# A decoder trunk on one core: the out-projections cut into sixteen more tiles, eight of them in the attention and SSD phases

## The reference

```python
up = rmsnorm(hp, norm_pre[i])
...
return (y * jax.nn.silu(gate)) @ w_out, bufs       # attention, y is 2048 wide
...
y = (yg.reshape(n, l, SSD_D_INNER) * norm_w.astype(jnp.float32)).astype(u.dtype)
return y @ w_out, h_new, conv_new                  # SSD, y is 2048 wide
...
hp = hp + rmsnorm(yp, norm_post[i])
```

## Time and profile before

| | us |
|---|---|
| runs, median of 3 (lowest, highest) | 1526.88 (1523.71, 1529.86) |
| the profiled execution's own time | 1523.6 |
| its span | 1521.8 |
| PE busy | 1368.0 (90%) |
| DVE busy | 815.2 (54%) |
| ACT busy | 670.8 (44%) |
| POOL busy | 454.4 (30%) |

### The profile page before, as it was taken

One profiled execution on the slowest core, in us unless ns is written; L12 is line 12 of the kernel. 1 busy time (PEld: TensorE's weight loads), 2 busy tenths in 40 slices (PEclk: granted clock), 3 DMA queues, 4 the chain that ended last, 5 costly groups with the idle time before them and its releaser, 6 DMA issues. The chain is left out here.

```text
span 1521.8 us, 29918 instructions
## 1 busy us (share of the span) xinstructions
PE 1368.0 (90%) x11182; PEld 1302.2 (86%) x11182; DVE 815.2 (54%) x1437; ACT 670.8 (44%) x1453; POOL 454.4 (30%) x393
## 2 busy tenths in 40 slices
PE   4999989999999998999966899499998989985996
PEld 4999879998899997999956899388897988874896
DVE  4444275443655445554443422667879769795323
ACT  3333433334434334343352432457566665743332
POOL 2545323453325442344420011002425143250011
PEclk8999999999999999999988899599999999997998
DMA  5562332623336233263421930443463735525711
GB/s 158 158 200 71 110 104 82 213 85 109 93 99 208 85 109 93 82 197 119 113 61 56 310 98 0 123 129 111 121 188 88 206 94 158 161 85 194 227 55 59
DMA packets 271172, 190.67 MB, mean 125 GB/s; under 512 B 10608, under 2 KB 258112, under 8 KB 270656
## 3 DMA queue, kind: packets, MB, share of 16 engines
q1 hardware_dynamic: 271040, 188.86, 41.5%
HBM read 159.92 MB, written 49.75 MB: 138 GB/s over the span
## 5 line engine op out<-in xcount | busy, mean ns | idle before, releaser
L1306 POOL TENSOR_TENSOR wlo<-w,whi 128x1024 fp32r<-128x1024 f32 x88 | 214.0, 2432 | 426.7 <-ACT whi L1001 426.7
L845 PE MATMUL at_proj<-uhi,whi 128*128 128x272 f32 x1408 | 310.8, 302 | 10.1 <-issue 6.1
L845 PE MATMUL at_proj<-uhi,wlo 128*128 128x272 f32 x1408 | 293.6, 290 | 0.0
L845 PE MATMUL at_proj<-ulo,whi 128*128 128x272 f32 x1408 | 293.3, 290 | 0.0
L845 PEld LDWEIGHTS at_proj<-uhi,whi 128*128 128x128 f32 x1408 | 221.6, 191 | 14.5 <-issue 7.4
L845 PEld LDWEIGHTS at_proj<-ulo,whi 128*128 128x128 f32 x1408 | 223.9, 191 | 0.0
L845 PEld LDWEIGHTS at_proj<-uhi,wlo 128*128 128x128 f32 x1408 | 222.9, 191 | 0.0
L1001 ACT ACTIVATE whi<-w 128x1024 fp32r<-128x1024 f32 x88 | 93.0, 1057 | 289.0 <-PE at_proj L845 272.1
L1740 PE MATMUL sd_proj<-uhi,sd_whi 128*128 128x272 f32 x640 | 143.7, 306 | 11.2 <-DVE sd_wlo L2134 11.2
L341 PE MATMUL m_acc<-m_yhi,m_whi 128*128 128x272 f32 x512 | 111.5, 300 | 35.8 <-DVE m_ylo L474 33.6
L1740 PE MATMUL sd_proj<-uhi,sd_wlo 128*128 128x272 f32 x640 | 134.5, 293 | 0.0
(11 more groups left out here) (296 smaller groups left out, 2517.4 us busy)
## 6 DMA issues: line engine op xcount, KB each, us to landing
w<-in_attn_w_in_dram SPq DMA_DIRECT2D x92, 512.0 KB, 4.0
sd_w<-in_ssd_w_in_dram SPq DMA_DIRECT2D x40, 512.0 KB, 4.4
m_rows<-mixed SPq DMA_DIRECT2D x32, 272.0 KB, 5.7
sd_h<-in_state_ssm_dram SPq DMA_DIRECT2D x16, 512.0 KB, 6.1
sd_bc<-acs_p SPq DMA_DIRECT2D x16, 512.0 KB, 5.3
out_s_ssm_dram<-sd_h SPq DMA_DIRECT2D x16, 512.0 KB, 3.1
m_w<-in_attn_w_out_dram SPq DMA_DIRECT2D x7, 1024.0 KB, 6.6
m_w<-in_ssd_w_out_dram SPq DMA_DIRECT2D x7, 1024.0 KB, 7.4
```

The lines of the kernel that those rows point to most:

```text
L845: last = pe.matmul(proj[:, r, h, 0:HALF], a[:, r, kk * P:(kk + 1) * P], b[:, kk, h * HALF:(h + 1) * HALF], start=(kk == 0 and a is whi and ...
L1306: pool.tensor_tensor(wlo[:, r], w[:, r], whi[:, r].bitcast(F32), ALU.subtract).then_inc(wlo_ready, 1)
```

## The change

Each out-projection is cut in two along its contraction. The first half, on the y of groups 0 and 1, becomes eight tiles of 1024 x 128 behind the projection stream: in attention as tiles of a group NG in the last stage, in SSD as tiles of kind "O". Their input is read back from `y_dram` into SBUF, split into `uhi` and `ulo` when the last projection is done (`split_high`, `split_low`; `YL`, `YH`), and their results stay in SBUF as `part`. In SSD `part` lies in the buffers `xbc` and `raw`. The second half, on groups 2 and 3, is done in `mix_phase`, with eight tiles of 48 products on the same ring. There DVE adds `part` in place of ACT's copy (`add_part`). Group 3's y (in SSD also group 2's) stays in SBUF and is neither stored nor loaded. The last tiles of each phase load and split the first two weight tiles of the next: those of the mix phases and, in `m1` on POOL, those of SSD. `all_groups` loops over two stages and writes the third out. The loops of `mix_phase` are written out. SSD's due times are new (two lines of the table are shown), and POOL now sums z of the last group as well.

```diff
 def all_groups(eng, plan, stage):
 
     stage(plan.first())
-    with eng.Fori(0, NG - 1) as i:
+    with eng.Fori(0, NG - 2) as i:
         stage(plan.middle(i))
+    stage(plan.middle(NG - 2))
     stage(plan.last())
...
+def out_tile(w_out, n):
+
+    k, o = divmod(n, KD)
+    return w_out.rearrange("(k p) n -> p k n", p=P)[:, KD * k:KD * (k + 1), o * P:(o + 1) * P]
...
+            for k in absent:
+                sp.dma_start(y[k], y_dram[KD + k]).then_inc(y_in, 16)
+            for o in range(PAIR, 2 * PAIR):
+                load_w(o)
...
+            for o in range(2 * PAIR, KD + more):
+                sp.wait_ge(wlo_ready, o - 1)
+                load_w(o)
...
+            for o in range(KD):
+                if o >= PAIR:
+                    pe.wait_ge(wlo_ready, o + 1)
+                    pe.wait_ge(fm_ready, o - 1)
+                products(o, 0)
+                if o:
+                    turn(o - 1)
+                products(o, 1)
+            turn(KD - 1)
...
+            for k in order:
+                if y_held[k] is None:
+                    act.wait_ge(y_in, 16 * len(absent))
+                act.activation(uhi[:, k, :], y[k], ACT.Copy).then_inc(yhi_ready, 1)
+            act.wait_ge(cleared, 2)
+            for o in range(KD):
+                if o + PAIR < KD + more:
+                    w_high(o + PAIR)
+                if o:
+                    square_rows(o - 1)
+            square_rows(KD - 1)
...
+                dve.tensor_tensor(two(fm[:, o % PAIR]), halves(acc[:, o % PAIR]), two(part[o]), ALU.add).then_inc(fm_ready, 1)
...
+            for o in range(KD):
+                if o:
+                    get_rows(o - 1)
+                add_part(o)
+                if o + PAIR < KD:
+                    w_low(o + PAIR)
...
+            for o in range(KD, KD + more):
+                pool.wait_ge(whi_ready, o - PAIR + 1)
+                pool.tensor_tensor(wlo[:, o % PAIR], w[:, o % PAIR], whi[:, o % PAIR].bitcast(F32), ALU.subtract) \
+                    .then_inc(next_low, 1)
...
+                    if isinstance(g, int) and g == NG - 1 and t == 8:
+                        sp.wait_ge(y_stored, 16 * 2)
+                        for j in range(KD):
+                            sp.dma_start(part[:, j, :], y_dram[j]).then_inc(y_in, 16)
...
+                    if isinstance(g, int) and g == NG and t == 0:
+                        pe.wait_ge(part_lo, kk + 1)
...
                         if st.head is not None:
                             project(st.head, t, q)
+                        elif t < KD:
+                            project(NG, t, q)
...
+            def out_projected(t):
+
+                act.wait_ge(proj_ready, TILES * NG + t + 1)
+                w_high(NG, t + PAIR)
+                act.activation(two(part[:, t, :]), halves(proj[:, t % PAIR]), ACT.Copy).then_inc(part_ready, 1)
+                act.wait_ge(part_ready, t + 1)
+                act.sem_inc(proj_free[t % PAIR], 1)
+
+            def split_high():
+
+                act.wait_ge(proj_ready, TILES * NG)
+                act.wait_ge(y_in, 16 * KD)
+                for j in range(KD):
+                    act.activation(uhi[:, j, :], part[:, j, :], ACT.Copy).then_inc(part_hi, 1)
...
+                for j in range(KD):
+                    pool.wait_ge(part_hi, j + 1)
+                    pool.tensor_tensor(ulo[:, j, :], part[:, j, :], uhi[:, j, :].bitcast(F32), ALU.subtract).then_inc(part_lo, 1)
...
+                if g is None:
+                    split_low()
+                    for t in range(KD):
+                        w_low(NG, t + PAIR)
...
+             [("O", None, o) for o in range(KD)])
...
-    (-16.5, ("SG", 0)), (-7, ("SG", 1)), (-6.5, ("CB",)), (-4.5, ("CS",)), (-3.5, ("TE",)), (-1, ("BC", 2)), (0, ("BS",)),
+    (-17.5, ("SG", 0)), (-7.5, ("SG", 1)), (-7.5, ("CB",)), (-4.5, ("CS",)), (-3.5, ("TE",)), (-0.5, ("BT",)), (0, ("CM",)),
...
-SCAN_LEN = (34, 34, 36, 34)
+SCAN_LEN = (34, 34, 34, 34)
...
+LOAD_AT = 138
+SPLIT_AT = (0.1, 0.3)
...
+                elif what == "YL":
+                    sp.wait_ge(y_stored, 32 * 2)
...
+                    for k in range(KD):
+                        sp.dma_start(part[k], y_dram[k]).then_inc(y_in, 16)
...
+                elif what == "YH":
+                    act.wait_ge(proj_ready, NIN)
+                    act.wait_ge(y_in, 16 * KD)
+                    act.activation(uhi[:, k, :], part[k], ACT.Copy).then_inc(part_hi, 1)
...
+                elif what == "YH":
+                    dve.wait_ge(part_hi, k + 1)
+                    dve.tensor_tensor(ulo[:, k, :], part[k], uhi[:, k, :].bitcast(F32), ALU.subtract).then_inc(part_lo, 1)
```

More of the change, by code:

```diff
@@ L327, in _, with products @@
             sp.wait_ge(stored, 16 * TT)
-            sp.wait_ge(x_in, 16 * TT)
         @block.tensor
         def _(pe):
[L333 to L339, removed]
+            def products(o, half):
+                r = o % PAIR
+                for n in range(KD // 2 * half, KD // 2 * (half + 1)):
+                    k = order[n]
+                    if o == 0:
+                        pe.wait_ge(ylo_ready, n + 1)
+                    for a, b in ((whi, uhi), (whi, ulo), (wlo, uhi)):
                         for h in range(2):
@@ L342, in products, with turn @@
                                              b[:, k, h * HALF:(h + 1) * HALF],
-                                             start=(k == 0 and a is whi and b is yhi),
-                                             stop=(k == KI - 1 and a is wlo))
-                if k1 == KI:
+                                             start=(n == 0 and a is whi and b is uhi),
+                                             stop=(n == KD - 1 and a is wlo))
+                if half == 1:
                     last.then_inc(acc_ready, 1)
-            def turn(o, r):
+            def turn(o):
+                r = o % PAIR
                 pe.wait_ge(fm_ready, o + 1)
-                if not isinstance(o, int) or o >= 2:
+                if o >= PAIR:
                     pe.wait_ge(rows_ready, o - 1)
@@ L356, in turn @@
                 last.then_inc(back_ready, 1)
[L358 to L367, removed]
-            tile(0, 0)
-            tile(1, 1)
-            with pe.Fori(0, KD // 2 - 1) as i:
-                tile(2 * i + 2, 0)
-                tile(2 * i + 3, 1)
-            turn(KD - 1, 1)
+            for o in range(KD):
+                if o >= PAIR:
+                    pe.wait_ge(wlo_ready, o + 1)
[5 more added lines that the diff above has]
+            turn(KD - 1)
             if pre is not None:
@@ L544, in _ @@
             pool.wait_ge(post_in, 16)
-            with pool.Fori(0, KD - 1) as o:
+            for o in range(KD - 1):
                 pool.wait_ge(squares, o + 1)
-                at = bass.ds(o * P, P)
+                at = slice(o * P, (o + 1) * P)
                 x = rows[:, 0:TT - 1, at]
@@ L1443, with out_parts, ssd_phase @@
 SSD_CONSTS = 6
-def ssd_phase(nc, uhi, ulo, ident, w_in_dram, tables, params, states, y_dram, p_out, s_out_dram, scratch):
+def out_parts(xbc, raw):
+    return [xbc[:, 0, o, :] for o in range(XBC)] + [raw[:, o, 0:TOK] for o in range(KD - XBC)]
+def ssd_phase(nc, uhi, ulo, ident, ring_w, held_sb, w_in_dram, w_out, tables, params, states, y_dram, p_out, s_out_dram, scratch):
+    w, whi, wlo = ring_w
+    xbc, raw, y = held_sb
+    part = out_parts(xbc, raw)
     conv_w, conv_b, dt_bias, a_log, d_skip, norm_w = params
@@ L1945, in tile @@
                     raw_out(i)
-                else:
-                    z_out(i)
-                if i + PAIR < NTILES:
-                    w_high(i + PAIR)
+                elif SSD_TILES[i][0] == "Z":
+                    z_out(i)
+                else:
+                    act.activation(two(part[i - NIN]), halves(proj[:, i % PAIR]), ACT.Copy).then_inc(part_ready, 1)
+                w_high(i + PAIR)
                 if SSD_TILES[i][0] == "C":
```

283 lines of the change are left out of this document (119 added, 164 removed), and 24 rows, old and new, of the table SCAN.

## The result

The changed kernel takes 1504.47 us (median of 4 runs, 1502.3 to 1507.92), 22 us less than the 1526.56 of the kernel before: ratio 0.9857, 95% interval 0.9828 to 0.9886. A second series of five runs gave 1502.38 (1501.22 to 1504.07), ratio 0.9844, interval 0.9831 to 0.9858. The forecast was 1498, with a range of 1487 to 1512. In the changed kernel, attention and SSD each hold eight of the new half tiles, sixteen in all; the title can be read as eight together.

What follows compares the result with a forecast made beforehand. PE was taken as busy nearly throughout the long stretches, with idle time and low clock in the seams. Gains 10.7 + 1.0 + 0 + 16.6 = 28.3 us gave 1495.3 on the profile's scale, 1498 for the runs; range 1487 to 1512.

Steps and rivals of the forecast that it cites:

- Seam 1: Attention and first mix, 782.8 to 947.7: last mix product at 937.0, gain 10.7 us, bounds 5 and 16.
- the 1.73 us of the slowed splits: Attention's last stage: four of POOL's eight splits take 1.73 us beside the merge chain, four 1.35 behind it.
- The bound of 5 us for late weights behind the eight reads: Weight load queued behind eight y reads, twice: costed at nothing, up to 5 us each without cover from tiles ahead.
- Seam 2: First mix to SSD, 947.7 to 981.6: PE no longer waits for load and split; gain 1.0 us, from -4 to +5.
- The loss to POOL beside the norm chain: First mix to SSD: POOL's two splits delay DVE's norm chain by 0 to 4.8 us, taken as 3.5.
- the 1.8 us counted back for SSD's setup: SSD's setup waits for DMAs that move ahead only about 1 to 3 us, so 1.8 us of gain is deducted.
- Seam 3: SSD and second mix, 1377.2 to 1507.2: last product at 1490.6, gain 16.6 us, bounds 10 and 20.
- SSD: SSD phase, 395.6 us: effect of the new table of due times taken as 0, between -8 and +8 us.
- the same items and nearly the same slots: Argument that SSD's new table would not make the kernel slower, against a rival of over 1535 us, chance 0.06.
- I count from fixed points: Whole kernel: the sum of products does not change, so only idle time and clock are won, counted from profiled times.
- The seams close fully: Rival, 1486 us: pauses cost no clock, POOL's splits run at 1.35, SSD's new table wins 5; chance 0.15.
- slow first tiles and SSD loses: Rival, 1512 us: POOL and DVE hinder each other (5 + 2), low clock (3), SSD's table costs 5; chance 0.13.

Runs made afterwards that it cites:

- b1: Changed kernel with ScalarE's copies to `uhi` ahead of the merge's exponential and POOL's eight splits ahead of its last weight split; 1502.09 us, ratio 0.9831.
- a4: Changed kernel with POOL's two weight splits for SSD issued earlier, at the last two tiles of the first mix phase; 1499.21 us, ratio 0.9823.
- a3: Changed kernel with SSD's due times (scan, gates, finish, parameters, setup) of the kernel before; 1500.87 us, ratio 0.9818.
- b0: The kernel before, unchanged, run once more for a second profile; one run, 1525.5 us.
- b2: Changed kernel with ScalarE's copies to `uhi` ahead of the merge's exponential and the eight splits on VectorE in place of POOL; 1501.78 us, ratio 0.9832.
- c2: Changed kernel with splits on VectorE behind ScalarE's early copies, POOL's early weight splits for SSD, and the merge's turned factors (F) later; 1490.36 us, ratio 0.9737.
- c3: The same three edits as c2, but the eight splits on POOL, ahead of its last weight split; 1491.61 us, ratio 0.9757.
- c1: Changed kernel with the merge's turned factors (F) behind OS 1 and one more quarter tile, in all stages; 1496.96 us, ratio 0.9805.

## Why the prediction was right, and where it was off

- **The total.** The time is 6.5 us above the forecast in the first series and 4.4 in the second. The mechanism, idle time in three seams filled by out tiles, is what the traces show. That the total held is in part the width of the range: two stretches that the sum had at nothing lost 9 to 14 us. The sum itself gives 1498.6 (1495.3 and 3.3), of which 1498 was made.
- **Seam 1.** Forecast from the last projection product to the last mix product 154.2 us, measured 153.3. The first out tile should end after 24.2 us, it did after 24.9; the last out product after 93.2, it was 92.0; the mix phase's first product 99.0, it was 98.2. Both the 1.73 us of the slowed splits and the low clock through the first tile were in it. Right. What it did not ask is whether the order on ScalarE and POOL, which sets where the splits begin, had to be kept (b1). The bound of 5 us for late weights behind the eight reads was not needed: PE is busy 119.87 of 120 us from 640 to 760, where they lie.
- **Seam 2.** The loss to POOL beside the norm chain was taken at 3.5 and is 4.1 (4.44 less 0.30); a4 removes it and wins 3.2 in time. It was looked for in the steps that read two SBUF tensors, and it fell on one that reads a single one. Measured gain 2.6 for 1.0, though that loss was larger: with the 4.1 it makes 6.7, where 6.3 less 1.8 were worked out. So the 1.8 us counted back for SSD's setup did not show here. SSD by the old table is 396.2 us behind the new seam (a3) and 392.5 to 395.4 behind the old one, so it may have shown there.
- **Seam 3.** Forecast 3.9 us from the last projection product to the first out product, measured 3.6; gain 15.5 for 16.6. The mix phase's first product comes 61.0 us after the last projection product, 59.5 were worked out, because the out tiles took 1.5 more.
- **SSD.** "I take 0, between -8 and +8" was 3.3 and 5.3 us lost against the profile that the forecast stood on, and 6.0 and 8.1 against b0. a3 shows that the table has a price in the scan and pays it back in seam 3, whose gain was thus partly the table's: a rule of "the same items and nearly the same slots" hides both.
- **The step that failed** is "I count from fixed points". It set the time up to 782.80 as equal, and never costed the third stage's move out of the loop. Its price is 2 to 3 us by five traces, and no more than 2.4 by the runs. The rest of the 5.7 to 9.1 us lies in the first stage, 205.5 and 208.9 us for 202.5. How much of it is luck is open: b0 ran 0.4 us under its median and has 201.3, so the forecast's lucky execution (3.3 us under) does not explain it alone.
- **Rivals.** "The seams close fully" did not come (POOL's splits slowed, and the granted clock is 0.66 from the last projection product to the first turn). Of "slow first tiles and SSD loses" the last part came (5.3 and 3.3 us of the 5), while splits and paced tile cost about what the forecast had in it.

## What to carry to other kernels

Cost not only the seams that a change aims at but every place where its code changes shape: here a stage written out of a loop was entered without the jump's pause, and then waited for what the pause had covered. Take a second profile before you count from fixed points: the two of the kernel before differ by 2.8 us in SSD and 3.4 in seam 1. When an engine is given earlier work (b2), look for the wait behind it; the earlier splits gained nothing measurable alone, on either engine, and 2 to 3 us once F stood later (c2 and c3 are 6.6 and 5.4 us below c1, 3 of them a4's edit), which is about what the runs can tell. Before a helper engine gets work beside a chain of small operations, ask if it can be done a tile earlier.

## What the runs showed of the hardware

- A VectorE operation of 128x5 elements with one SBUF input lasted 4.44 us beside two POOL splits of together 4.62, and 0.30 in a4. It stood for both splits, not for one. The 0.30 has a remnant of the same: it began at 944.87 and ended at 945.17, and POOL's operation beside it ended at 945.14; with POOL idle, in the kernel before, it lasted 0.17. The Trainium skill, "SBUF — State Buffer", section "Who interferes with whom", names `tensor_scalar` among the operations that can take the port pair shared with GpSimd, and says that the one that comes second is then fully blocked. The trace agrees, but for the second split.
- POOL's splits of 128x544 took 1.33 or 1.34 us beside VectorE's reciprocal (one input) and 1.78 to 2.32 beside its `tensor_tensor` steps (up to 2.84 in b1); a 4x512 step of the merge took 0.68 alone and 1.70 to 2.76 beside POOL.
- With the same code there, PE waits 3.6 us for the first stage's F in four profiles and 2.0 in seven, and the granted clock from 200 to 230 us, of this wait and the products around it, lies between 0.77 and 0.94. With F later it is 0.94, 0.94 and 1.00 (c1, c2, c3). The clock does not follow the length of the wait: 0.94 with 3.6 us (before), 0.77 with 2.0 (b1). What sets it in one execution is not shown, nor how much of the scatter between runs comes from it.
